# GpSimd computes the low halves of the down weights in the FFN stages and the experts, in place of VectorE

## The chip, the cores and the metric

The program runs on one NeuronCore of a Trainium2 chip. The metric is the device time of one execution in microseconds (us), taken as the median over several executions. TensorE is called PE here, VectorE DVE, ScalarE ACT, GpSimd POOL, and SP is the engine whose queue issues most of the loads.

## The reference

Two transformer-like blocks run one after the other over 256 tokens of width 1024. What matters here is their feed-forward part, which occurs four times as one dense FFN (twice in layer 0 of the first block, for the tokens and for the context; once in its layer 1; once in the second block) and once as a mixture of eight experts.

```python
def swiglu(h, wg, wu, wd):                      # FFN_DIM = 2816, in the second block 3584
    return (jax.nn.silu(h @ wg) * (h @ wu)) @ wd

def moe_swiglu(h, router_w, w_gate, w_up, w_down):
    ...
    top_v, top_i = lax.top_k(logits, TOP_K)
    top_p = jax.nn.softmax(top_v, axis=-1)
    gates = jnp.sum(jax.nn.one_hot(top_i, N_EXPERTS) * top_p[..., None], axis=1)
    for e in range(N_EXPERTS):                  # 8 experts, each 1024 -> 3584 -> 1024
        out = out + gates[:, e:e + 1] * swiglu_2(t, w_gate[e], w_up[e], w_down[e])
```

All inputs are fp32.

## The kernel before

**Chunks.** The hidden dimension of an FFN is cut into chunks of 128. One chunk needs 1.5 MB of fp32 weights: 128x1024 of the gate matrix, 128x1024 of the up matrix (together the "front" of a ring slot, 1 MB) and 128x1024 of the down matrix (the "back", 512 KB). The ring `RING` (in the trace: `weights`) has four slots. SP loads front and back in turn, and waits before each for the semaphore `front_used` or `back_used`, which says that the slot's old content has been read for the last time. The FFNs have 22, 22, 22 and 28 chunks, 94 together; the experts have 28 chunks each, 224 together.

**Splitting.** PE does not multiply the fp32 weights. Each is written as a sum of two bf16 numbers, high + low, and a product takes three bf16 passes (high x high, high x low, low x high). ACT makes the high half by a copy to bf16 (`cast_hi`; in the loops `cast_hi_loop`, lines 792 and 795), DVE the low half by subtracting the bf16 high half from the fp32 weights (`make_lo`): line 624 for gate and up together, 128x2048, and line 628 for down, 128x1024. The split weights have two buffers each, by the parity of the chunk. In the trace they are called `normed_or_mix` and `aux`.

**One step of the loop, chunk c.** PE does `up_products(c+1)` (lines 639 to 641, 48 matmuls), then `down_products(c)` (lines 654 to 656). In the experts the tokens of one expert are gathered to 128 columns, in the dense FFNs there are 256. ACT does the silu of chunk c (line 662), then the high half of gate and up of chunk c+2, then the high half of down of chunk c+1. DVE does `gate_of(c)`: the product of silu and up (line 669), its bf16 high half (line 677) and its low half (line 679); then `make_lo` of gate and up of chunk c+2, then `make_lo` of down of chunk c+1. `down_products(c)` waits for `back_used`, raised by the low half of down, and for `act_done`, raised by line 679. After 28 chunks of an expert DVE copies its output out of PSUM (`keep_output`, line 900) and PE adds it to the sum (line 852).

**Order.** Each engine's order is written out by hand, one instruction after another; there is no scheduler. The loop bodies hold four chunks, one for each ring slot. In the layout of the data line 624 and line 679 read two tensors from SBUF (weights and high half; hidden values and their high half), line 669 reads one from SBUF and one from PSUM, line 677 one from SBUF.

GpSimd has no instruction in these stages before the change. The experts are built twice, for up to 128 tokens in an expert (`moe_parts`) and for more (`ffn_parts` with gates), and a number counted on the chip chooses; in this case the first is run.

Of the kernel before, what the change touches and what calls it, by code (L numbers as in the profile page):

```python
# [21 lines left out]
ALU = mybir.AluOpType  # L22
# [3 lines left out]
D, T, PB = 1024, 256, 128  # L26
# [3 lines left out]
SLOT, SLOTS = KD * WC, 4  # L30
# [52 lines left out]
class Place:  # L83


    n = 0
# [57 lines left out]
def build(nc, ctx, d, out):  # L144
# [47 lines left out]
    S = Signals(sig)  # L192
# [426 lines left out]
    def make_lo(dve, which, j, n):  # L619

        s = (place.n + j) % SLOTS
        if which == 0:
            dve.wait_ge(S.hi_gu.sem, n + S.hi_gu.at(1))
            dve.tensor_tensor(gu[parity(j)][1], RING[:, s, 0:2 * D], gu[parity(j)][0],  # L624
                              ALU.subtract).then_inc(front_used.sem, 1)
        else:
            dve.wait_ge(S.hi_d.sem, n + S.hi_d.at(1))
            dve.tensor_tensor(split[parity(j)][2][1], RING[:, s, 2 * D:3 * D], split[parity(j)][2][0],  # L628
                              ALU.subtract).then_inc(back_used.sem, 1)

    def up_products(pe, j, n, hid, width, h_hi, h_lo):

# [49 lines left out]
    def ffn_done(n):  # L682
        place.n += n
        for s in (S.up_done, S.down_done, S.act_done, S.prod):
            s.done(n + 2)
        for s in (S.silu_done, S.act_hi, S.hi_gu, S.hi_d):
            s.done(n)

    def ffn_parts(x, f, o, gates=None):

        a, n = place.n, f // PB * (NE if gates is not None else 1)
        hid = [PS[:, 4 + p, :] for p in range(2)]
        h_hi, h_lo = (P[:, i * 1024:(i + 1) * 1024].bitcast(BF16).rearrange("p (k t) -> p k t", k=KD)
                      for i in range(2))
        h = HT[:, :, o:o + T]
        outs = ((0, (0, 1)), (1, (2, 3)))
        rounds = (n - 2) // SLOTS

        def products(pe):
            for bank in range(4):
                pe.matmul(PS[:, bank, :], Z16[:, 0:PB], Z16[:, :], start=True, stop=False)
            pe.sem_inc(S.up_done.sem, 2)
            pe.sem_inc(S.down_done.sem, 2)
            pe.wait_ge(S.hop_d.sem, S.hop_d.at(2))

            def up(j, n):
                up_products(pe, j, n, hid, T, lambda k: h_hi[:, k, :], lambda k: h_lo[:, k, :])
            up(0, 0)  # L710
            with pe.Fori(0, rounds) as g:
                for j in range(SLOTS):
                    up(j + 1, g * SLOTS + (j + 1))
                    down_products(pe, j, g * SLOTS + j, outs)
            for c in range(rounds * SLOTS, n):
                if c + 1 < n:
                    up(c + 1, c + 1)
                down_products(pe, c, c, outs, stop=(c == n - 1))

        def silus(act):  # L720
            act.activation(h_hi, h, ACT.Copy).then_inc(S.hop_d.sem, 1)
            cast_hi(act, 0, 0, 0)
            cast_hi(act, 0, 1, 1)
            cast_hi(act, 1, 0, 0)
            with act.Fori(0, rounds) as g:
                for j in range(SLOTS):
                    silu_of(act, j, g * SLOTS + j, hid, T)
                    cast_hi_loop(act, 0, j + 2, g, 0)
                    cast_hi_loop(act, 1, j + 1, g, 0)
            for c in range(rounds * SLOTS, n):  # L730
                silu_of(act, c, c, hid, T)
                if c + 2 < n:
                    cast_hi(act, 0, c + 2, c + 2)
                if c + 1 < n:
                    cast_hi(act, 1, c + 1, c + 1)

        def gating(dve):
            dve.sem_inc(S.act_done.sem, 2)
            dve.sem_inc(S.prod.sem, 2)
            dve.wait_ge(S.hop_d.sem, S.hop_d.at(1))  # L740
            dve.tensor_tensor(h_lo, h, h_hi, ALU.subtract).then_inc(S.hop_d.sem, 1)
            make_lo(dve, 0, 0, 0)
            make_lo(dve, 0, 1, 1)
            make_lo(dve, 1, 0, 0)
            if gates is None:
                with dve.Fori(0, rounds) as g:
                    for j in range(SLOTS):
                        gate_of(dve, j, g * SLOTS + j, hid, T)
                        make_lo(dve, 0, j + 2, g * SLOTS + (j + 2))
                        make_lo(dve, 1, j + 1, g * SLOTS + (j + 1))  # L750
                for c in range(rounds * SLOTS, n):
                    gate_of(dve, c, c, hid, T)
                    if c + 2 < n:
                        make_lo(dve, 0, c + 2, c + 2)
                    if c + 1 < n:
                        make_lo(dve, 1, c + 1, c + 1)
            else:
                fc = f // PB
                def steps(e, j, c, more=2):
                    gate_of(dve, j, c, hid, T, gates[:, bass.ds(e, 1), :].rearrange("p o t -> p (o t)"))  # L760
                    if more > 1:
                        make_lo(dve, 0, j + 2, c + 2)
                    if more > 0:
                        make_lo(dve, 1, j + 1, c + 1)
                with dve.Fori(0, NE - 1) as e:
                    with dve.Fori(0, fc // SLOTS) as g:
                        for j in range(SLOTS):
                            steps(e, j, e * fc + g * SLOTS + j)
                with dve.Fori(0, fc // SLOTS - 1) as g:
                    for j in range(SLOTS):  # L770
                        steps(NE - 1, j, g * SLOTS + ((NE - 1) * fc + j))
                for j in range(SLOTS):
                    steps(NE - 1, j, n - SLOTS + j, SLOTS - 1 - j)
            dve.wait_ge(S.down_done.sem, S.down_done.at(n + 2))
            for b in range(2):
                for h_ in range(2):
                    t = AUX[:, (2 * b + h_) * 512:(2 * b + h_ + 1) * 512]
                    dve_step(dve, dve.tensor_tensor(t, PS[:, 2 * b + h_, :], GB[:, h_ * 512:(h_ + 1) * 512], ALU.mult))
                    xo = x[:, b, h_ * 512:(h_ + 1) * 512]
                    dve.tensor_tensor(xo, xo, t, ALU.add)  # L780
        return products, silus, gating
# [15 lines left out]
    def ffn(x, f, o):  # L797

        a, n = place.n, f // PB
        products, silus, gating = ffn_parts(x, f, o)  # L800
        with nc.Block() as block:
            @block.sync
            def _(sp):
                feed(sp, a + SLOTS, a + n + SLOTS)

            @block.tensor
            def _(pe):
                products(pe)

            @block.scalar  # L810
            def _(act):
                silus(act)

            @block.vector
            def _(dve):
                gating(dve)
        ffn_done(n)
        S.hop_d.done(2)

    def moe_parts(he_hi, he_lo, put_t, fc):  # L820
# [69 lines left out]
        def gating(dve):  # L890
            def step(j, c, more=2):
                gate_of(dve, j, c, hid, PB)
                if more > 1:
                    make_lo(dve, 0, j + 2, c + 2)
                if more > 0:
                    make_lo(dve, 1, j + 1, c + 1)

            def keep_output(e):
                dve.wait_ge(S.down_done.sem, e * fc + S.down_done.at(fc + 2))
# [2 lines left out]
            dve.sem_inc(S.prod.sem, 2)  # L902
            make_lo(dve, 0, 0, 0)
            make_lo(dve, 0, 1, 1)
            make_lo(dve, 1, 0, 0)
            with dve.Fori(0, NE - 1) as e:
                with dve.Fori(0, fc // SLOTS) as g:
                    for j in range(SLOTS):
# [397 lines left out]
    for layer in range(2):  # L1306
# [476 lines left out]
        with nc.Block() as block:  # L1783
            @block.sync
            def _(sp):
                feed(sp, a + SLOTS, a + n + SLOTS)

            @block.tensor
            def _(pe):
                few = pe.value_load(COUNT[0:1, 0:1], min_val=0, max_val=T) <= PB  # L1790
                with pe.If(few):
                    gathered[0](pe)
                with pe.Else():
                    general[0](pe)

            @block.scalar
            def _(act):
                few = act.value_load(COUNT[0:1, 0:1], min_val=0, max_val=T) <= PB
                with act.If(few):
                    gathered[1](act)  # L1800
                with act.Else():
                    general[1](act)

            @block.vector
            def _(dve):
                few = dve.value_load(COUNT[0:1, 0:1], min_val=0, max_val=T) <= PB
                steps = dve_step.n
                with dve.If(few):
                    gathered[2](dve)
                dve_step.n = steps  # L1810
                with dve.Else():
                    general[2](dve)
        ffn_done(n)
        checkpoint(nc, "s1", X)

# [163 lines left out]
```

## Time and profile before

| | |
|---|---|
| median of 3 executions | 3390.8 us (3386.8 to 3391.04) |
| the profiled execution, its own time | 3383.39 us |
| its span, first to last instruction | 3381.6 us |
| mean granted TensorE clock | 0.893 |
| busy PE / DVE / ACT / POOL | 2904.6 / 1989.6 / 1411.8 / 0.2 us |
| experts, first to last line 624 | 2358.12 to 3344.36 us |
| HBM read | 674.71 MB |

The profile's rows give the start of an instruction, its duration, engine, line, operation, output<-inputs with their shapes, and in brackets how long the engine sat idle before it and what ended the idle time. Successive DVE instructions overlap by some 0.08 us in these rows, since one starts while the last results of the one before are written. So the distance from start to start says what an instruction costs its engine.

### The profile page before, as it was taken

How to read it: one execution, taken by the hardware profiler on the slowest of the kernel's cores; microseconds unless marked ns; L12 is line 12 of the kernel's file. 1: busy time of each engine (PE TensorE's matmuls, PEld its weight loads, DVE VectorE, ACT ScalarE, POOL GpSimd, SP SyncE). 2: the span in 40 equal slices, each digit the busy share in tenths (PEclk: the TensorE clock that was granted, in tenths of full speed). 3: DMA queues.
4: the chain of work that ended last, by engine and by line, in shares of the span. 5: the costliest groups of instructions: out<-in, count | busy, mean ns of one | idle time of the engine just before them, and what ended most of it. 6: DMA issues, size and time to landing. Idle time of an engine off the chain costs nothing. (4 is left out here: it accounts for less than half of the span.)

```text
span 3381.6 us, 59663 instructions
## 1 busy us (share of the span) xinstructions
PE 2904.6 (86%) x22985; PEld 2098.9 (62%) x23302; DVE 1989.6 (59%) x3126; ACT 1411.8 (42%) x1705; POOL 0.2 (0%) x4
## 2 busy tenths in 40 slices
PE   5879979999786777989668989767999999999997
PEld 3446657667453545766446766445777777777775
DVE  2234345555325553551446551445999999999997
ACT  1124124344123422430314430311777777777775
POOL 0000000000000000000000000000000000000000
PEclk8968789999887787999679999577999999999999
DMA  5440036455244204643424543320999999999995
GB/s 238 151 180 1 19 129 215 159 190 195 84 165 175 111 29 145 215 173 135 165 97 170 198 169 143 143 106 24 347 349 368 350 347 353 363 348 351 366 349 193
DMA packets 124090, 677.25 MB, mean 200 GB/s; under 512 B 13808, under 2 KB 14288, under 8 KB 69200
## 3 DMA queue, kind: packets, MB, share of 16 engines
q1 hardware_dynamic: 122256, 664.80, 53.0%
q10 hardware_dynamic: 1728, 11.01, 0.9%
q8 instruction: 70, 1.15, 0.1%
q14 instruction: 36, 0.29, 0.0%
HBM read 674.71 MB, written 1.05 MB: 200 GB/s over the span
## 5 line engine op out<-in xcount | busy, mean ns | idle before, releaser
L639 PE MATMUL ps<-projected,normed_or_mix 128*128 (+2 forms) x5088 | 1032.7, 236 | 46.8 <-DVE normed_or_mix L624 22.7
L640 PE MATMUL ps<-projected,normed_or_mix 128*128 (+2 forms) x5088 | 1030.5, 236 | 0.0
L639 PEld LDWEIGHTS ps<-projected,normed_or_mix 128*128 128x128 bf16 x5088 | 499.3, 98 | 173.5 <-DVE normed_or_mix L624 66.7
L792 ACT ACTIVATE normed_or_mix<-weights 128x2048 bf16<-128x2048 f32 x304 | 578.5, 1903 | 0.0
L640 PEld LDWEIGHTS ps<-projected,normed_or_mix 128*128 128x128 bf16 x5088 | 499.8, 98 | 33.0
L641 PE MATMUL ps<-projected,normed_or_mix 128*128 (+2 forms) x2544 | 519.0, 237 | 0.0
L641 PE MATMUL ps<-projected,aux 128*128 (+2 forms) x2544 | 510.9, 235 | 0.0
L551 PE MATMUL ps<-weights,turned 128*128 128x384 f32 (+3 forms) x1440 | 444.4, 472 | 17.7 <-PEq L420 7.2
L624 DVE TENSOR_TENSOR normed_or_mix<-weights,normed_or_mix 128x2048 bf16<-128x2048 f32 x159 | 364.0, 2289 | 48.9 <-ACT normed_or_mix L792 40.7
L551 PEld LDWEIGHTS ps<-weights,turned 128*128 128x128 f32 x1440 | 275.5, 194 | 185.9 <-issue 31.6
L624 DVE TENSOR_TENSOR aux<-weights,normed_or_mix 128x2048 bf16<-128x2048 f32 x159 | 363.7, 2287 | 28.2 <-ACT normed_or_mix L792 27.6
L662 ACT ACTIVATE probs<-ps 128x128 f32<-128x128 f32 (+1 forms) x318 | 97.8, 308 | 481.9 <-PE ps L641 481.1
L669 DVE TENSOR_TENSOR probs_turned<-probs,ps 128x128 f32<-128x128 f32 (+1 forms) x318 | 102.7, 323 | 269.1 <-ACT probs L662 269.1
L641 PEld LDWEIGHTS ps<-projected,normed_or_mix 128*128 128x128 bf16 x2544 | 251.1, 99 | 9.9
L641 PEld LDWEIGHTS ps<-projected,aux 128*128 128x128 bf16 x2544 | 248.9, 98 | 8.5
L628 DVE TENSOR_TENSOR aux<-weights,aux 128x1024 bf16<-128x1024 f32 x159 | 193.9, 1220 | 8.5 <-ACT aux L617 8.5
L628 DVE TENSOR_TENSOR normed_or_mix<-weights,normed_or_mix 128x1024 bf16<-128x1024 f32 x159 | 194.0, 1220 | 0.0
L335 PE MATMUL ps<-weights,silu_cond 128*32 128x384 f32 x1024 | 138.3, 684 | 43.6 <-DMA weights<-ada 14.5
L963 ACT ACT_TABLE_LOAD x30 | 38.5, 1283 | 322.7 <-PEq L537 203.5
L795 ACT ACTIVATE normed_or_mix<-weights 128x1024 bf16<-128x1024 f32 x152 | 159.9, 1052 | 19.6 <-PE ps L656 19.6
L795 ACT ACTIVATE aux<-weights 128x1024 bf16<-128x1024 f32 x152 | 159.4, 1049 | 11.1 <-PE ps L656 11.1
L655 PE MATMUL ps<-normed_or_mix,probs 128*128 128x512 bf16 x412 | 156.1, 379 | 8.6 <-DVE probs L679 0.3
(319 smaller groups left out, 3483.1 us busy)
## 6 DMA issues: line engine op xcount, KB each, us to landing
weights<-moe SPq DMA_DIRECT2D x224, 1024.0 KB, 7.1
weights<-moe SPq DMA_DIRECT2D x224, 512.0 KB, 7.2
weights<-l_ffn SPq DMA_DIRECT2D x66, 1024.0 KB, 5.1
weights<-ada SPq DMA_DIRECT2D x64, 1024.0 KB, 5.7
weights<-l_ffn SPq DMA_DIRECT2D x66, 512.0 KB, 5.5
weights<-ada SPq DMA_DIRECT2D x64, 512.0 KB, 6.5
weights<-ffn SPq DMA_DIRECT2D x28, 1024.0 KB, 4.9
weights<-w_in SPq DMA_DIRECT2D x16, 1024.0 KB, 5.8
```

Of the source, the lines that this page charges most:

```text
L335: mm = pe.matmul(PS[32 * j:32 * (j + 1), 5 + i % 2, 0:WC], CS[:, k, :], RING[:, (a + i) % SLOTS, k * WC:(k + 1) * WC], start=(turn_ == 0), ...
L551: mm = pe.matmul(PS[:, q % 8, 0:w], src(k)[:, b * PB:(b + 1) * PB], RING[:, slot, k * w:(k + 1) * w], start=(k == 0), stop=(k == kt - 1))
L624: dve.tensor_tensor(gu[parity(j)][1], RING[:, s, 0:2 * D], gu[parity(j)][0], ALU.subtract).then_inc(front_used.sem, 1)
L628: dve.tensor_tensor(split[parity(j)][2][1], RING[:, s, 2 * D:3 * D], split[parity(j)][2][0], ALU.subtract).then_inc(back_used.sem, 1)
L639: pe.matmul(o, hi, h_hi(k), start=(k == 0), stop=False)
L640: pe.matmul(o, hi, h_lo(k), start=False, stop=False)
L641: mm = pe.matmul(o, lo, h_hi(k), start=False, stop=(k == KD - 1))
L655: pe.matmul(PS[:, bank, :], hi[:, o], w_lo[:, c], start=False, stop=False)
L662: act.activation(silu[parity(j)][:, 0:width], hid[parity(j)][:, 0:width], ACT.Silu).then_inc(S.silu_done.sem, 1)
L669: dve.tensor_tensor(f, silu[p][:, 0:width], hid[p][:, T:T + width], ALU.mult).then_inc(S.prod.sem, 1)
L792: act.activation(gu[parity(j)][0], RING[:, s, 0:2 * D], ACT.Copy).then_inc(S.hi_gu.sem, 1)
L795: act.activation(split[parity(j)][2][0], RING[:, s, 2 * D:3 * D], ACT.Copy).then_inc(S.hi_d.sem, 1)
```

## The change

The low half of the down weights is made by GpSimd in a loop of its own (`down_lows`), with the same operands, buffers, semaphore waits and signals. DVE's `make_lo` keeps only gate and up. It applies to the four dense FFNs (`ffn`), and to the experts, in both their forms.

```diff
     def make_lo(dve, which, j, n):
 
         s = (place.n + j) % SLOTS
-        if which == 0:
-            dve.wait_ge(S.hi_gu.sem, n + S.hi_gu.at(1))
-            dve.tensor_tensor(gu[parity(j)][1], RING[:, s, 0:2 * D], gu[parity(j)][0],
-                              ALU.subtract).then_inc(front_used.sem, 1)
-        else:
-            dve.wait_ge(S.hi_d.sem, n + S.hi_d.at(1))
-            dve.tensor_tensor(split[parity(j)][2][1], RING[:, s, 2 * D:3 * D], split[parity(j)][2][0],
-                              ALU.subtract).then_inc(back_used.sem, 1)
+        dve.wait_ge(S.hi_gu.sem, n + S.hi_gu.at(1))
+        dve.tensor_tensor(gu[parity(j)][1], RING[:, s, 0:2 * D], gu[parity(j)][0],
+                          ALU.subtract).then_inc(front_used.sem, 1)
+
+    def down_lows(pool, n):
+        def low(j, c):
+            s = (place.n + j) % SLOTS
+            pool.wait_ge(S.hi_d.sem, c + S.hi_d.at(1))
+            pool.tensor_tensor(split[parity(j)][2][1], RING[:, s, 2 * D:3 * D], split[parity(j)][2][0],
+                               ALU.subtract).then_inc(back_used.sem, 1)
+
+        with pool.Fori(0, n // SLOTS) as g:
+            for j in range(SLOTS):
+                low(j, g * SLOTS + j)
+        for c in range(n // SLOTS * SLOTS, n):
+            low(c, c)
...
@@ -741,27 +749,21 @@
             make_lo(dve, 0, 0, 0)
             make_lo(dve, 0, 1, 1)
-            make_lo(dve, 1, 0, 0)
...
@@ -814,6 +816,10 @@
+
+            @block.gpsimd
+            def _(pool):
+                down_lows(pool, n)
...
@@ -892,8 +898,6 @@
                 gate_of(dve, j, c, hid, PB)
                 if more > 1:
                     make_lo(dve, 0, j + 2, c + 2)
-                if more > 0:
-                    make_lo(dve, 1, j + 1, c + 1)
```

In DVE's order at the experts before, the end of the prologue and the first step of the loop stand so (`probs` and `probs_turned` are the hidden values and their halves):

```order
L624 TENSOR_TENSOR normed_or_mix<-weights,normed_or_mix 128x2048
L624 TENSOR_TENSOR aux<-weights,normed_or_mix 128x2048
L628 TENSOR_TENSOR normed_or_mix<-weights,normed_or_mix 128x1024
L906 UNCONDITIONAL_BRANCH
L907 UNCONDITIONAL_BRANCH
L907 ISA
L669 TENSOR_TENSOR probs_turned<-probs,ps 128x128
L670 REGISTER_ALU
L676 REGISTER_ALU
L677 CAST probs<-probs_turned 128x128
L679 TENSOR_TENSOR probs<-probs_turned,probs 128x128
```

After the change the same place of DVE's order reads as follows; the new lines 623, 677, 685 and 687 are the old 624, 669, 677 and 679.

```order
L623 TENSOR_TENSOR normed_or_mix<-weights,normed_or_mix 128x2048
L623 TENSOR_TENSOR aux<-weights,normed_or_mix 128x2048
L909 UNCONDITIONAL_BRANCH
L910 UNCONDITIONAL_BRANCH
L910 ISA
L677 TENSOR_TENSOR probs_turned<-probs,ps 128x128
L678 REGISTER_ALU
L684 REGISTER_ALU
L685 CAST probs<-probs_turned 128x128
L687 TENSOR_TENSOR probs<-probs_turned,probs 128x128
L622 REGISTER_ALU
L623 TENSOR_TENSOR normed_or_mix<-weights,normed_or_mix 128x2048
```

The 128x1024 subtraction is gone from DVE, in the prologue and in each step, and nothing has taken its place. On POOL, which had no rows here, the loop of the experts is this:

```order
L633 ISA
L630 TENSOR_TENSOR normed_or_mix<-weights,normed_or_mix 128x1024
L629 REGISTER_ALU
L630 TENSOR_TENSOR aux<-weights,aux 128x1024
L629 REGISTER_ALU
L630 TENSOR_TENSOR normed_or_mix<-weights,normed_or_mix 128x1024
L629 REGISTER_ALU
L630 TENSOR_TENSOR aux<-weights,aux 128x1024
L633 REGISTER_ALU
L633 COMPARE_AND_BRANCH
```

So POOL holds all down subtractions of a stage, in the order of the chunks, and each waits only for ACT's high half of the same chunk.

## Rows read from the trace of the kernel before

**Rows 1.** The page's busy time, share of the span and instructions of each engine.

```profile
PE 2904.6 (86%) x22985; PEld 2098.9 (62%) x23302; DVE 1989.6 (59%) x3126; ACT 1411.8 (42%) x1705; POOL 0.2 (0%) x4
```

**Rows 2.** Busy time by window (dense FFN, experts), then clock, DMA share, GB/s.

```profile
500.00:560.00 60.00, 59.58 (x456) 45.17 (x462) 36.37 (x40) 28.22 (x27) 0.00 (x0) 1.00 0.58 203
...
2400.00:2480.00 80.00, 76.70 (x994) 59.58 (x1012) 76.40 (x96) 63.23 (x62) 0.00 (x0) 1.00 0.97 368
```

**Rows 3.** Timeline of DVE in the experts: one full step, and a later one.

```profile
2801.26 2.28 DVE L624 TENSOR_TENSOR normed_or_mix<-weights,normed_or_mix 128x2048 bf16<-128x2048 f32 x1
2803.46 1.22 DVE L628 TENSOR_TENSOR aux<-weights,aux 128x1024 bf16<-128x1024 f32 x1
2804.60 0.28 DVE L669 TENSOR_TENSOR probs_turned<-probs,ps 128x128 f32<-128x128 f32 x1
2804.91 0.23 DVE L677 CAST probs<-probs_turned 128x128 bf16<-128x128 f32 x1
2805.18 0.29 DVE L679 TENSOR_TENSOR probs<-probs_turned,probs 128x128 bf16<-128x128 f32 x1
2805.38 2.29 DVE L624 TENSOR_TENSOR aux<-weights,normed_or_mix 128x2048 bf16<-128x2048 f32 x1
...
2809.96 2.29 DVE L624 TENSOR_TENSOR normed_or_mix<-weights,normed_or_mix 128x2048 bf16<-128x2048 f32 x1 [0.28 <-ACT normed_or_mix L792]
```

**Rows 4.** Who waited for whom between 2400 and 3300 us: total, times, longest.

```profile
ACT probs L662 <- PE ps L641: 162.0, 109, 4.9
...
PEld ps L639 <- DVE normed_or_mix L624: 55.7, 80, 1.1
...
DVE normed_or_mix L624 <- ACT normed_or_mix L792: 15.6, 44, 0.7
```

**Rows 5.** Waits of SP's queue between 2400 and 3300 us.

```profile
SPq L226 <- DVE normed_or_mix L624: 274.9, 101, 3.8
```

**Rows 6.** Timeline of PE in the experts: two starts of up products, down products.

```profile
2799.48 0.23 PE L639 MATMUL ps<-projected,normed_or_mix 128*128 x1
...
2803.25 0.38 PE L656 MATMUL ps<-normed_or_mix,probs 128*128 128x512 bf16 x1
2803.60 0.23 PE L639 MATMUL ps<-projected,normed_or_mix 128*128 x1
...
2810.71 0.38 PE L655 MATMUL ps<-normed_or_mix,probs 128*128 128x512 bf16 x1
...
2812.31 0.23 PE L639 MATMUL ps<-projected,normed_or_mix 128*128 x1 [0.36 <-DVE normed_or_mix L624]
```

**Rows 7.** Timeline of DVE: the first and the last line 624 of the experts.

```profile
2358.12 2.29 DVE L624 TENSOR_TENSOR normed_or_mix<-weights,normed_or_mix 128x2048 bf16<-128x2048 f32 x1 [7.68 <-ACT normed_or_mix L614]
...
3344.36 2.28 DVE L624 TENSOR_TENSOR aux<-weights,normed_or_mix 128x2048 bf16<-128x2048 f32 x1
```

**Rows 8.** Timeline of DVE at the end of an expert.

```profile
2859.82 1.22 DVE L900 COPY aux<-ps 128x1024 f32<-128x1024 f32 x1
...
2867.94 0.29 DVE L669 TENSOR_TENSOR probs_turned<-probs,ps 128x128 f32<-128x128 f32 x1 [2.67 <-ACT probs L662]
...
2869.74 2.29 DVE L624 TENSOR_TENSOR aux<-weights,normed_or_mix 128x2048 bf16<-128x2048 f32 x1 [0.83 <-ACT normed_or_mix L792]
```

**Rows 9.** Timeline of ACT in the experts.

```profile
2804.35 1.05 ACT L795 ACTIVATE normed_or_mix<-weights 128x1024 bf16<-128x1024 f32 x1
2806.56 1.28 ACT L662 ACT_TABLE_LOAD   x1 [1.16 <-PE ps L641]
```

**Rows 10.** Timeline of DVE in a dense FFN: the halves of 256 columns.

```profile
512.72 0.29 DVE L677 CAST probs<-probs_turned 128x256 bf16<-128x256 f32 x1
513.05 0.43 DVE L679 TENSOR_TENSOR probs<-probs_turned,probs 128x256 bf16<-128x256 f32 x1
```

**Rows 11.** Window at the program's start: DMA share and GB/s last.

```profile
10.00:15.00 5.00, 2.56 (x16) 0.45 (x8) 0.00 (x0) 0.49 (x1) 0.00 (x0) 1.00 1.01 425
```

**Rows 12.** The page's DMA issues: KB each, median us to landing.

```profile
weights<-moe SPq DMA_DIRECT2D x224, 1024.0 KB, 7.1
```

More of the change, by code:

```diff
@@ L749, in gating @@
                         make_lo(dve, 0, j + 2, g * SLOTS + (j + 2))
-                        make_lo(dve, 1, j + 1, g * SLOTS + (j + 1))
                 for c in range(rounds * SLOTS, n):
@@ L754, in gating @@
                         make_lo(dve, 0, c + 2, c + 2)
-                    if c + 1 < n:
-                        make_lo(dve, 1, c + 1, c + 1)
             else:
@@ L894, in step @@
                     make_lo(dve, 0, j + 2, c + 2)
-                if more > 0:
-                    make_lo(dve, 1, j + 1, c + 1)
             def keep_output(e):
@@ L904, in gating @@
             make_lo(dve, 0, 1, 1)
-            make_lo(dve, 1, 0, 0)
             with dve.Fori(0, NE - 1) as e:
@@ L1812, in _ @@
                     general[2](dve)
+            @block.gpsimd
+            def _(pool):
+                down_lows(pool, n)
         ffn_done(n)
```

## The prediction

> **What bounds the kernel now.** I read the busy times by window first. In a dense FFN PE is busy 59.6 of 60 us and DVE 36.4; in the experts DVE is busy 76.4 of 80 us, PE 76.7, and the DMA share is 0.97 [rows 2]. So the two kinds of stage have different limits, and the reader should look at the experts, where three resources look full. The timeline of DVE settles which one it is: a step takes 4.12 us from line 624 to line 624, and DVE never stops in it: 2.20 us from line 624 to 628, 1.14 to 669, 0.31 to 677, 0.27 to 679, 0.20 to the next 624 [rows 3]. PE, in contrast, starts its up products at 2799.48 and again at 2803.60, and its last down matmul starts at 2803.25, some 0.22 us before PE could go on; its own work is 3.99 us of the 4.12 [rows 6]. The table of waits says the same: PE waits for DVE's line 624 80 times, ACT waits for PE, and nobody waits for a DMA [rows 4]. SP waits 274.9 us for line 624 [rows 5], so the ring is full of loads that arrive early and the high DMA share is a rate set by DVE. At the program's start the same queue moved 425 GB/s, at which 1.5 MB (1.57 million bytes) take 3.70 us [rows 11, 12].
>
> The mean distance of two lines 624 in the experts is more: 986.2 us over 223 steps, 4.42 us [rows 7]. Of the 0.30 us above 4.12, 0.14 come from ACT's table load: one step in four, the next line 624 comes 4.58 us after the one before, as 2805.38 + 4.58 = 2809.96, and the step in front of it takes 0.10 longer as well [rows 3, 9]. The remaining 0.16 us a step, 36 us in all, is what the ends of seven experts cost: the copy of 1.22 us and idle times of 2.67 and 0.83 us [rows 8].
>
> **What the change removes.** DVE loses 94 + 224 = 318 subtractions of 128x1024. In the dense FFNs PE has no gap to close, so their 94 are worth nothing. In the experts a step of DVE falls by 1.14 to 2.98 us.
>
> **What it adds.** The same subtraction on GpSimd, which computes nothing before (4 instructions, 0.2 us) [rows 1]. Its price is not in this trace. The lower bound is DVE's own 1.22 us [rows 3]. As upper bound I take twice that, 2.44 us, and as value 2.29 us, the time of the subtraction of twice the size on DVE [rows 3]; this is a choice, made near the upper end because nothing here shows GpSimd to be as fast as the engine made for such work.
>
> The Trainium skill, GPSIMD Engine Reference, section 3.1, gives 4497 ns for a 2048-column fp32 subtraction's sister, the add, on GpSimd, against 2293 ns on DVE; half of it is 2.25 us. DVE's 2.29 us for 2048 columns agrees; no run here shows GpSimd's. With 2.25 the sum below would be 9 us lower.
>
> **Where it lies.** If the two engines did not disturb each other, 2.29 us would be hidden. ACT finishes the down half at 2804.35 + 1.05 = 2805.40, and the down products that read it start at 2810.71 [rows 6, 9]: 5.31 us of room. The signal for the ring would come about a microsecond later than now, against loads that land 7.1 us after issue with four slots of over 4 us each [rows 12]; ACT has not waited for one.
>
> The open question is whether they disturb each other, and the trace has no place where both work. The bounds are 0 and the whole length of GpSimd's instruction in every step. Two things in the rows speak for the upper end. Lines 624 and 679, 2.49 of DVE's 2.98 us, read two tensors from SBUF. And line 677, which reads one, grows by only 0.06 us (0.23 to 0.29) for 128 more columns, where line 679 grows by 0.14 [rows 3, 10]: DVE has a second path into SBUF and uses it in both kinds. GpSimd must read two tensors too, from the same partitions. I take the upper end: while GpSimd's subtraction runs, lines 624, 677 and 679 wait, and the reverse.
>
> The Trainium skill, SBUF — State Buffer, section "Who interferes with whom", states just this: a DVE instruction with two SBUF inputs contends with a GpSimd instruction that reads SBUF, and the second to start blocks fully. No run here shows it yet. By it the change is slower; without it, faster (below).
>
> **The sum.** A step becomes 2.98 + 2.29 = 5.27 us. Line 669, which has one input in PSUM, could run beside GpSimd, which would give 4.96; but ACT issues the down half after gate and up (0.95 us later), so that GpSimd's turn comes late in line 624 or behind 669. I keep 5.27. The table load disappears: ACT already idles 1.16 us before it [rows 9], and with a step 1.15 us longer it fits. The ends of the experts keep their 36 us. So 223 x 5.27 + 36 = 1211 us in place of 986: +225 us. In a dense FFN DVE's step would be 2.98 + 0.35 (for 256 columns in place of 128, from line 679 and 677 and as much as line 679 again for line 669) + 2.29 = 5.6 us; PE needs 7.8 (60 us hold 7.7 such steps, with PE at 59.6 of 60), so the taking of turns is hidden under PE: 0. If that cover were gone, each 0.1 us a chunk would cost 9 us. Prologues: 0, since the first down subtraction has the first up products beside it.
>
> Against its own time of 3383.4 us this gives 3608; the median of the runs is 0.2% higher, which makes 3616. I say 3612 us, 6.5% slower.
>
> Bounds: with 2.44 us and 0.1 us for each of two hand-overs a step is 5.62 us and the sum +303, 3694 us. With 4.96 us a step it is +156, 3547. With GpSimd at 1.5 us it is 4.48 us a step and +49 to +80, depending on whether the table load is hidden, so about 3450.
>
> **The rivals.**
> *No disturbance, PE next.* DVE's 2.98 us fit easily, and PE sets 3.99 us a step. Once in four steps the table load shows: from its start at 2806.56, when PE had just finished its up products, to the start of the up products two chunks on, 2812.31, are 5.75 us [rows 6, 9], against 3.99 + 1.3 us of PE's own work between (down, up, down): 0.46 us, 0.12 a step. 223 x 4.11 + 36 = 953 us, -33: 3358 us, 1.0% faster. The load rate is no obstacle (3.70 us). For it: the 5.31 us of room. Against it: the second input of line 624.
> *GpSimd is the bound by itself,* undisturbed but slow. It decides from 4.26 us on (the mean step inside an expert now), and at 4.6 us costs 223 x 0.34, some +75 us: 3466. Against it: it is nearly four times DVE's time.
> *Partial disturbance, or a short GpSimd instruction.* At 1.22 us and taking turns a step is 4.20 us: +18 us, 3409. If GpSimd slipped into DVE's gaps and only stretched its instructions, the 1.14 us come back as about 1.14 us: no change.
>
> **How the numbers follow.** Taking turns at about 2.3 us: 0.72, with a range of its own from 3540 to 3700. Partial, or short: 0.08, of which 0.05 no change, the rest slower. GpSimd the bound: 0.04. PE next: 0.16. A measurement of this kernel can tell some 0.2% from no change. That makes faster 0.16, same 0.05, slower 0.79. The range goes from 3450 to 3710: it leaves out the faster case and most of the near-neutral ones.
>
> **What would show it.** Line 623 (now 624) starting every 5.0 to 5.6 us in the experts, with idle time or a longer duration on lines 623, 685 and 687 next to a GpSimd instruction; no start of one inside the other's run. PE's busy share there falls to about 3.99 of 5.3, and the DMA rate to near 300 GB/s. The dense FFNs keep 7.8 us a chunk. I am wrong if line 623 starts every 4.0 us with GpSimd running beneath it; or if GpSimd's instructions come back to back.

## The result, and the profile after

The changed kernel takes 3501.4 us (median of 4 runs, 3500.1 to 3508.0) against 3390.9 us before: a ratio of 1.0331, 95% interval 1.0305 to 1.0357, 110 us slower. The forecast was slower, 3612 us in a range of 3450 to 3710. The direction and the mechanism held; the size was twice what was measured.

First the page after, busy time by engine and the lines that answer to the ones shown of before (line 623 is the old 624, 677 the old 669, 685 the old 677, 687 the old 679).

```profile
PE 2909.9 (83%) x22985; PEld 2119.8 (61%) x23302; DVE 1977.1 (56%) x2808; ACT 1416.6 (40%) x1705; POOL 1016.2 (29%) x322
...
L630 POOL TENSOR_TENSOR normed_or_mix<-weights,normed_or_mix 128x1024 bf16<-128x1024 f32 x159 | 455.4, 2864 | 1962.7 <-ACT normed_or_mix L617 1661.4
L630 POOL TENSOR_TENSOR aux<-weights,aux 128x1024 bf16<-128x1024 f32 x159 | 562.5, 3537 | 487.6 <-ACT aux L797 458.6
```

The same trace's groups, with the shapes kept apart, give the cast of the experts alone:

```profile
L685 DVE CAST probs<-probs_turned 128x128 bf16<-128x128 f32 x224 | 266.9, 1191 | 17.3
```

DVE has 318 instructions fewer, and yet it is busy for 1977.1 us, 12.5 us less than before, where 318 x 1.14 = 363 us were taken away. Its cast of 128 columns, which took 0.23 us [rows 3], has a mean of 1191 ns. Its work did not grow; the cast waits inside its own span.

The windows of the same stretches as in [rows 2] show where the loss is.

```profile
500.00:560.00 60.00, 59.58 (x452) 44.69 (x458) 28.74 (x32) 28.22 (x27) 23.73 (x8) 1.00 0.59 209
2400.00:2480.00 80.00, 64.61 (x849) 51.31 (x864) 68.33 (x65) 53.24 (x53) 45.58 (x17) 1.00 0.84 314
```

In the dense FFN PE is as busy as before, 59.58 of 60 us. In the experts PE falls from 76.70 to 64.61 of 80 us and the loads from 368 to 314 GB/s. From its first to its last line 623 the experts' stage takes 3459.89 - 2367.27 = 1092.6 us, where it took 986.2 [rows 7]: +106.4 us, nearly the whole difference.

The timeline of DVE and of POOL in the experts, one round of four steps, shows the mechanism instruction by instruction.

```profile
2800.14 2.29 DVE L623 TENSOR_TENSOR aux<-weights,normed_or_mix 128x2048 bf16<-128x2048 f32 x1 [0.84 <-ACT normed_or_mix L794]
2802.35 0.28 DVE L677 TENSOR_TENSOR probs_turned<-probs,ps 128x128 f32<-128x128 f32 x1
2802.66 1.85 DVE L685 CAST probs<-probs_turned 128x128 bf16<-128x128 f32 x1
2804.54 0.29 DVE L687 TENSOR_TENSOR probs<-probs_turned,probs 128x128 bf16<-128x128 f32 x1
2804.75 2.28 DVE L623 TENSOR_TENSOR normed_or_mix<-weights,normed_or_mix 128x2048 bf16<-128x2048 f32 x1
2806.95 0.28 DVE L677 TENSOR_TENSOR probs_turned<-probs,ps 128x128 f32<-128x128 f32 x1
2807.27 1.85 DVE L685 CAST probs<-probs_turned 128x128 bf16<-128x128 f32 x1
2809.15 2.20 DVE L687 TENSOR_TENSOR probs<-probs_turned,probs 128x128 bf16<-128x128 f32 x1
2811.27 2.28 DVE L623 TENSOR_TENSOR aux<-weights,normed_or_mix 128x2048 bf16<-128x2048 f32 x1
...
2814.34 2.28 DVE L623 TENSOR_TENSOR normed_or_mix<-weights,normed_or_mix 128x2048 bf16<-128x2048 f32 x1
```

```profile
2801.13 3.29 POOL L630 TENSOR_TENSOR normed_or_mix<-weights,normed_or_mix 128x1024 bf16<-128x1024 f32 x1 [6.83 <-ACT normed_or_mix L797]
2805.11 3.93 POOL L630 TENSOR_TENSOR aux<-weights,aux 128x1024 bf16<-128x1024 f32 x1 [0.68 <-ACT aux L797]
2809.08 2.12 POOL L630 TENSOR_TENSOR normed_or_mix<-weights,normed_or_mix 128x1024 bf16<-128x1024 f32 x1
2814.44 4.18 POOL L630 TENSOR_TENSOR aux<-weights,aux 128x1024 bf16<-128x1024 f32 x1 [3.24 <-ACT aux L797]
```

Read the ends, not the starts. GpSimd's second instruction is issued at 2805.11, inside line 623, which ends at 2807.03; it ends at 2809.04, 2.01 us after line 623. Beside it line 677 runs in its usual 0.28 us. The cast, issued at 2807.27, ends at 2809.12, right behind GpSimd. GpSimd's third subtraction was ready by then (ACT's high half of it ended at 2809.01) and is issued at 2809.08, ahead of DVE's line 687, which ends at 2811.35, behind GpSimd's 2811.20. This third one, which had nothing to wait for, gives GpSimd's own time: 2.12 us. The two engines take turns by whole instructions, and line 677, with one input in PSUM, is exempt. The Trainium skill, SBUF — State Buffer, section "Who interferes with whom", states that rule for two-input instructions and for casts at double rate; the trace agrees on both.

The steps from line 623 to line 623 in this round are 4.61, 6.52, 3.07 and 4.60 us. The second holds two of GpSimd's turns, the third none. This pattern repeats in the experts 2 to 8, with 18.72 us for most rounds; the first expert has another, shown further down. PE waits for DVE in all this and not for GpSimd itself: between 2400 and 3300 us its down products wait 70.2 us for line 687, and GpSimd's line 630 released PE's weight load once in the whole trace, after 1.7 us. No engine waits for a load there.

### The profile page after: what moved, and what is told of

Same layout as the page of the kernel before. It is cut to its first block and busy times, and to the rows that moved or that the text cites. A ratio compares the mean times of both kernels' runs of the same rounds, so it can differ in the third digit from the quotient of the medians.

```text
span 3499.7 us, 60146 instructions
## 1 busy us (share of the span) xinstructions
PE 2909.9 (83%) x22985; PEld 2119.8 (61%) x23302; DVE 1977.1 (56%) x2808; ACT 1416.6 (40%) x1705; POOL 1016.2 (29%) x322
## 5 line engine op out<-in xcount | busy, mean ns | idle before, releaser
L630 POOL TENSOR_TENSOR normed_or_mix<-weights,normed_or_mix 128x1024 bf16<-128x1024 f32 x159 | 455.4, 2864 | 1962.7 <-ACT normed_or_mix L617 1661.4
L630 POOL TENSOR_TENSOR aux<-weights,aux 128x1024 bf16<-128x1024 f32 x159 | 562.5, 3537 | 487.6 <-ACT aux L797 458.6
L623 DVE TENSOR_TENSOR normed_or_mix<-weights,normed_or_mix 128x2048 bf16<-128x2048 f32 x159 | 390.7, 2457 | 37.6 <-ACT normed_or_mix L794 29.2
L685 DVE CAST probs<-probs_turned 128x128 bf16<-128x128 f32 (+1 forms) x318 | 299.0, 940 | 23.4
L663 PE MATMUL ps<-aux,probs 128*128 128x512 bf16 x412 | 156.2, 379 | 89.2 <-DVE probs L687 84.0
L687 DVE TENSOR_TENSOR probs<-probs_turned,probs 128x128 bf16<-128x128 f32 (+1 forms) x318 | 206.2, 648 | 10.9
```

What stands on the lines that cost most here:

```text
L630: pool.tensor_tensor(split[parity(j)][2][1], RING[:, s, 2 * D:3 * D], split[parity(j)][2][0], ALU.subtract).then_inc(back_used.sem, 1)
L663: pe.matmul(PS[:, bank, :], hi[:, o], w_lo[:, c], start=False, stop=False)
L685: dve.tensor_copy(hid_hl[p][0][:, 0:width], f).then_inc(S.act_hi.sem, 1)
L687: dve.tensor_tensor(hid_hl[p][1][:, 0:width], f, hid_hl[p][0][:, 0:width], ALU.subtract).then_inc(S.act_done.sem, 1)
```

## The experiments

Twelve kernels were run, each beside runs of the kernel before on the same chip; the ratio is taken against those. "Step" is the distance of two of DVE's 128x2048 subtractions in the experts, "stage" the stretch from the first to the last of them, before 986.2 us. The stage is the sharper measure, since the program ahead of it varies: the experts begin anywhere between 2357 and 2391 us in the profiles, with no order by kernel.

**One column.** GpSimd keeps its place and its signals, but subtracts only one column; the low half of the other 1023 is set to zero once ahead of each stage's loop.

```diff
-            pool.tensor_tensor(split[parity(j)][2][1], RING[:, s, 2 * D:3 * D], split[parity(j)][2][0],
-                               ALU.subtract).then_inc(back_used.sem, 1)
...
+            w_hi, w_lo = split[parity(j)][2]
+            pool.tensor_tensor(w_lo[:, 0:1], RING[:, s, 2 * D:2 * D + 1], w_hi[:, 0:1], ALU.subtract).then_inc(back_used.sem, 1)
...
+        for p in range(2):
+            pool.memset(split[p][2][1][:, 1:D], 0.0)
```

> The kernel after the change, but GpSimd subtracts only column 0 of the down weights; the other 1023 columns of the low half stay zero, so that part of the product is left out. All waits and signals between the engines stay. Theory (the two engines take turns, GpSimd's work of 2.0 us is the price): with nothing to take turns over, PE is next, 4.0 to 4.1 us a step in the experts, 3350 to 3370 us. Rival (the way over GpSimd, its waits and signals, costs the time): still 3450 to 3500 us.

Measured: 3366.4 us, ratio 0.9926 (0.9900 to 0.9952), stage 961.6 us. The loss is gone with GpSimd's columns, so it is not the way over GpSimd. This is also the nearest measurement of the forecast's rival in which PE is next: it gave -33 us, the run shows -24.6 us in the stage. Even an instruction of one column takes its turn, as two rows of this run's timeline show:

```profile
2799.35 2.29 DVE L623 TENSOR_TENSOR aux<-weights,normed_or_mix 128x2048 bf16<-128x2048 f32 x1 [0.90 <-ACT normed_or_mix L796]
```

```profile
2800.34 1.35 POOL L631 TENSOR_TENSOR normed_or_mix<-weights,normed_or_mix 128x1 bf16<-128x1 f32 x1 [2.62 <-ACT normed_or_mix L799]
```

It is issued at 2800.34 and ends at 2801.69, just behind line 623, which ends at 2801.64.

**A write, a cast.** Behind the one column GpSimd fills the other 1023 with zeros, or casts the fp32 weights into them.

```diff
+            pool.memset(w_lo[:, 1:D], 0.0).then_inc(back_used.sem, 1)
```

> As the one-column kernel, but GpSimd then writes zeros to the other 1023 columns: a long GpSimd instruction that writes SBUF and reads none; the low half is left out of the product. Theory in its form that only reads collide with two-input instructions: lines of DVE's 128x2048 subtraction and of the hidden low half are not lengthened; DVE's cast, which runs at twice the rate, may be, by up to the length of the write (1 us or so). 3350 to 3400 us. Rival (any GpSimd work holds DVE): DVE's 128x2048 subtraction starts late too, 3420 us or more.

```diff
+            pool.tensor_copy(w_lo[:, 1:D], RING[:, s, 2 * D + 1:3 * D]).then_inc(back_used.sem, 1)
```

> As the one-column kernel, but GpSimd then casts the other 1023 columns of the fp32 weights to bf16 into the low half, one input in place of two; the low half of the product is wrong by that. Theory: it reads SBUF, so it and DVE take turns as in the changed kernel, for as long as it runs; a one-input instruction should be shorter, 1.0 to 1.3 us, so a step of 3.0 - 0.3 + 1.2 = 3.9 us is under PE's 4.0: 3355 to 3410 us, with the cast and the low half of DVE lengthened. Rival (two GpSimd inputs are what collides): no DVE instruction is lengthened.

Measured: 3368.8 us (0.9925, 0.9900 to 0.9951) and 3365.3 us (0.9918, 0.9886 to 0.9950). The write takes 0.94 us and the cast 1.03 us, and both fit under PE (stages of 961.8 and 961.7 us). DVE's cast waits for either, in 161 of the 224 steps of the experts. In the run with the write:

```profile
2803.90 0.78 DVE L686 CAST probs<-probs_turned 128x128 bf16<-128x128 f32 x1
```

```profile
2803.65 0.94 POOL L632 MEMSET aux<- 128x1023 bf16 x1
```

The cast ends at 2804.68, GpSimd's write at 2804.59. So against DVE's cast at double rate GpSimd need not read anything. Whether DVE's two-input subtraction would have let the write or the one-input cast pass was not seen: both always began when it had ended, since the one column in front of them had waited for it. That part of the two expectations stays untested.

**The high half from PSUM.** The changed kernel, with DVE's cast replaced by a product that reads PSUM; and as a control the kernel before with the same edit.

```diff
+        if gate is None:
+            dve.wait_ge(S.down_done.sem, n + S.down_done.at(1))
+            dve.tensor_tensor(hid_hl[p][0][:, 0:width], silu[p][:, 0:width], hid[p][:, T:T + width],
+                              ALU.mult).then_inc(S.act_hi.sem, 1)
...
-        dve.wait_ge(S.down_done.sem, n + S.down_done.at(1))
-        dve.tensor_copy(hid_hl[p][0][:, 0:width], f).then_inc(S.act_hi.sem, 1)
```

> The kernel after the change, but in the dense FFNs and the experts DVE makes the bf16 high half of the hidden values by a second product of silu (SBUF) and up (PSUM) in place of the cast from SBUF; same values. Theory: an instruction with one SBUF input that is not at double rate passes beside GpSimd, so only line 687's 0.2 us and the 128x2048 subtraction's 2.2 us take turns with GpSimd's 2.0: steps of 4.4 us in place of 4.6, 3440 to 3475 us, although DVE has 0.05 us more work a step. Rival (GpSimd holds every DVE instruction, or slows all by bandwidth): 3500 to 3515 us.

> The kernel before with the bf16 high half of the hidden values made from silu and PSUM in place of the cast, as in the run before that did so with GpSimd. Theory: DVE's step grows by 0.05 us or less, 3390 to 3405 us, so that the 3547 us of that run are due to how DVE and GpSimd meet, not to the other instruction by itself. Rival (the second product is costly by itself): 3430 us or more.

Measured: 3546.6 us (1.0464, 1.0413 to 1.0514), a clear miss, and for the control 3381.0 us (0.9960, 0.9926 to 0.9994). The rows of the run with GpSimd tell what was right and what was not:

```profile
2872.86 0.28 DVE L679 TENSOR_TENSOR probs<-probs,ps 128x128 bf16<-128x128 f32 x1
2873.05 0.28 DVE L681 TENSOR_TENSOR probs_turned<-probs,ps 128x128 f32<-128x128 f32 x1
2873.37 1.71 DVE L692 TENSOR_TENSOR probs<-probs_turned,probs 128x128 bf16<-128x128 f32 x1
2875.01 4.21 DVE L623 TENSOR_TENSOR aux<-weights,normed_or_mix 128x2048 bf16<-128x2048 f32 x1
```

```profile
2871.64 3.30 POOL L630 TENSOR_TENSOR aux<-weights,aux 128x1024 bf16<-128x1024 f32 x1 [2.04 <-ACT aux L802]
2874.89 2.18 POOL L630 TENSOR_TENSOR normed_or_mix<-weights,normed_or_mix 128x1024 bf16<-128x1024 f32 x1
```

Both products with PSUM pass beside GpSimd unhindered, and the step that meets one turn of GpSimd is 4.36 us, as expected (4.4). But most rounds are 4.36 + 6.27 + 4.62 + 5.33 = 20.6 us. The 6.27 us are a matter of order: GpSimd's next subtraction was ready before its last one had ended, was issued at 2874.89 and went ahead of line 623, which took 4.21 us, and line 623 is what PE waits for. In the step of 5.33 us the table load is exposed: DVE idles 1.33 us ahead of its first product.

The step of 4.62 us has another cause, TensorE's clock. PE idled 2.13 us, until line 623 ended, and started its up products at 2879.28. Half a microsecond later the granted clock in PE's rows is 0.50, the level of 1.2 GHz, and a matmul takes 0.31 us in place of 0.22; by 2884.80 it is back at 1.00, 2.4 GHz. The windows show it (PEclk is the number behind the brackets of POOL):

```profile
2879.80:2883.00 3.20, 3.20 (x33) 3.20 (x31) 3.20 (x2) 0.00 (x0) 1.41 (x1) 0.50 0.81 266
2884.80:2887.50 2.70, 2.70 (x49) 2.61 (x47) 1.72 (x2) 2.02 (x2) 0.60 (x1) 1.00 0.90 291
```

In the experts of this run 1272 up matmuls took more than 0.28 us; in every other run 26 to 56 did, all in the first expert. In each expert at least one round with the same order of turns but no slow matmul in its first step takes 19.33 us; those with them take 20.58. So the clock costs 1.25 us a round, in 31 of the 55 rounds: an estimate of 39 us, the ends of the experts left aside. That leaves some 3508 us for the order of the turns, still above the expected 3475. The expectation had neither: the sum of a step alone does not give the time.

The order is not a matter of this edit alone. The first expert of the changed kernel has it too: GpSimd goes ahead of line 623, and a step later DVE idles for the table load.

```profile
2427.97 4.22 DVE L623 TENSOR_TENSOR normed_or_mix<-weights,normed_or_mix 128x2048 bf16<-128x2048 f32 x1
2436.81 0.29 DVE L677 TENSOR_TENSOR probs_turned<-probs,ps 128x128 f32<-128x128 f32 x1 [1.63 <-ACT probs L670]
```

```profile
2427.83 2.22 POOL L630 TENSOR_TENSOR aux<-weights,aux 128x1024 bf16<-128x1024 f32 x1 [2.90 <-ACT aux L797]
```

There a round is 20.05 us in place of 18.72, with PE at full clock. What puts one expert in one pattern and the next in the other is not shown. The control shows that the edit itself is a gain: DVE's steps are 4.06 us, where 4.12 to 4.17 were expected, as the second product starts 0.20 us after the first where the cast started 0.31 us after it.

**Each stage alone.** The change in the experts only, and in the dense FFNs only (`down_lows` in one kind of stage, `make_lo` for both halves in the other).

> The change in the experts alone; the dense FFNs keep the down subtraction on DVE. Theory (the loss is in the experts, where DVE has no room): as the changed kernel, 3490 to 3510 us. Rival (part of the loss is in the dense FFNs or in loading GpSimd's code there): some 10 us or more below it.

> The change in the four dense FFNs alone. Theory: GpSimd takes turns with DVE there as well, but under PE's 7.8 us a chunk: as before within 0.2%, 3384 to 3398 us, with the cast lengthened all the same. Rival: the difference of 9 us ahead of the experts between the two profiles is real and belongs to the FFNs, 3400 us or more.

Measured: 3499.9 us (1.0269, 1.0209 to 1.0329), and 3391.9 us (0.9979, 0.9946 to 1.0013). The stages are 1092.4 and 986.4 us, so all of the loss belongs to the experts. The expectation and the prediction had DVE held in the dense FFNs as well, with PE's longer work covering it. It is hardly held at all: in the changed kernel one cast of 94 takes 1.77 us (at 504.01) and three more are longer than 0.30, and no other line of DVE's loop is lengthened; it is GpSimd that waits, 2.7 us being its usual duration in place of 2.12. DVE is idle 24 of 60 us there even before [rows 2], and GpSimd's turns fall into that time. The stretches from the first to the last 128x2048 subtraction are 351.7, 157.9 and 205.6 us against 351.7, 158.2 and 204.5 before (the first holds two FFNs).

**Two halves.** Each of GpSimd's subtractions is cut into two of 128x512.

```diff
...
+            pool.tensor_tensor(w_lo[:, 0:512], RING[:, s, 2 * D:2 * D + 512], w_hi[:, 0:512], ALU.subtract)
+            pool.tensor_tensor(w_lo[:, 512:D], RING[:, s, 2 * D + 512:3 * D], w_hi[:, 512:D],
                                ALU.subtract).then_inc(back_used.sem, 1)
```

> The changed kernel with each of GpSimd's subtractions cut into two of 128x512. Theory: the turn is per instruction, so DVE never waits longer than about 1.05 us for one GpSimd instruction where it now waits up to 1.9; the sum of GpSimd's time stays, 2.0 to 2.2 us a step, so the total stays within 3470 to 3530 us. Rival (bandwidth shared, no turns): no change in how DVE's instructions are lengthened.

Measured: 3467.7 us (1.0178, 1.0119 to 1.0237), just under the expected interval, stage 1058.9 us. DVE's waits have the new length:

```profile
2802.46 0.87 DVE L687 CAST probs<-probs_turned 128x128 bf16<-128x128 f32 x1
2803.36 1.15 DVE L689 TENSOR_TENSOR probs<-probs_turned,probs 128x128 bf16<-128x128 f32 x1
2804.44 3.25 DVE L623 TENSOR_TENSOR aux<-weights,normed_or_mix 128x2048 bf16<-128x2048 f32 x1
```

The cast waits 0.64 us, the low half 0.86, line 623 0.97. A turn is an instruction, and cutting it gives DVE places to get in.

**A share for GpSimd.** DVE subtracts the first 896, or 512, of the 1024 columns and its signal starts GpSimd on the rest, so that GpSimd's turn falls on the product from PSUM.

```diff
+            dve.tensor_tensor(w_lo[:, 0:896], RING[:, s, 2 * D:3 * D - 128], w_hi[:, 0:896],
+                              ALU.subtract).then_inc(S.lo_d.sem, 1)
...
+            pool.wait_ge(S.lo_d.sem, c + S.lo_d.at(1))
+            pool.tensor_tensor(w_lo[:, 896:D], RING[:, s, 3 * D - 128:3 * D], w_hi[:, 896:D],
+                               ALU.subtract).then_inc(back_used.sem, 1)
```

> GpSimd subtracts only the last 128 of the 1024 columns of the down weights, in all stages, and starts when DVE has done the first 896, so that its turn falls on line 669's product, which reads one input from PSUM and passes beside it. Theory: GpSimd's instruction takes 0.3 to 0.35 us, DVE's step falls from 4.12 to between 3.98 and 4.1 us, where PE's 3.99 takes over: 3366 to 3392 us. Rival (any use of GpSimd here costs more than it gives): 3395 us or more.

> As the run with 128 columns, with 512 of the 1024 on GpSimd. Theory: GpSimd's instruction takes 1.0 to 1.1 us, of which 0.3 lie beside the product from PSUM; DVE's step is 2.98 + 0.6 + 0.8 = 4.4 us, some 60 us more than before in the experts less up to 31 us of table loads that become hidden: 3415 to 3460 us. Rival (no turns, GpSimd hidden): below 3375 us.

Measured: 3387.6 us (0.9986, 0.9974 to 0.9998), steps of 4.12 us, stage 980.9 us, and 3432.0 us (1.0121, 1.0100 to 1.0143), steps of 4.45 us with no table load to be seen, stage 1022.1 us. With 512 columns GpSimd's 1.16 us lengthen most casts from 0.23 to 1.00 us or more; what DVE saves by the columns, 0.54 us, is less. With 128 nearly all of the 0.14 us saved is used up: GpSimd's 0.43 us reach past the product, and nine casts in ten have 0.27 to 0.36 us. A round is 16.95 us where it was 17.04, the 5 us of the stage.

**Both.** The share and the product from PSUM together, with 128 and with 256 columns on GpSimd.

> GpSimd subtracts the last 128 columns of the down weights, started by DVE's first 896, and DVE makes the bf16 high half of the hidden values from silu and PSUM in place of the cast. Theory: GpSimd's instruction of 0.43 us now lies beside two products that read PSUM, 0.5 us together, and costs DVE at most 0.1 us; DVE's step is 4.06 - 0.14 + 0.08 = 4.0 us, at PE's 3.99. With the table loads as in the one-column kernel: 3362 to 3376 us, faster than the kernel before and than the control without GpSimd (3381 us). Rival (a share for GpSimd gives nothing even so, as with 128 columns and the cast): 3378 to 3395 us.

> As the run with 128 columns and the product from PSUM, with 256 columns on GpSimd. Theory: GpSimd takes 0.65 us and begins 0.15 us after the first product, so that 0.3 us stick out and hold the low half; DVE's step is 4.06 - 0.28 + 0.3 = 4.08 us, no better than the control without GpSimd: 3372 to 3390 us, slower than 128 columns. Rival (turns cost little for short instructions): as fast as 128 columns or faster.

Measured: 3368.5 us (0.9951, 0.9929 to 0.9972) and 3368.8 us (0.9930, 0.9910 to 0.9950). Both beat the kernel before; the two cannot be told apart, and 256 columns did better than expected. With 128:

```profile
2805.15 0.28 DVE L687 TENSOR_TENSOR probs<-probs,ps 128x128 bf16<-128x128 f32 x1
2805.35 0.28 DVE L689 TENSOR_TENSOR probs_turned<-probs,ps 128x128 f32<-128x128 f32 x1
2805.66 0.29 DVE L700 TENSOR_TENSOR probs<-probs_turned,probs 128x128 bf16<-128x128 f32 x1
```

```profile
2805.31 0.43 POOL L638 TENSOR_TENSOR aux<-weights,aux 128x128 bf16<-128x128 f32 x1 [4.44 <-DVE aux L630]
```

GpSimd's subtraction lies from 2805.31 to 2805.74 under the two products, and line 700 still has its usual 0.29 us. The steps are 3.93 us three times in four, with 4.87 for the one with the table load; with 256 columns line 700 has 0.47 us and the steps are 3.97 us, with 4.73. A round is 16.66 us in both, and the same with one column: DVE's turns with GpSimd no longer set it, and that is why 256 columns are no worse. The stages are 965.6 and 966.5 us, against 975.5 in the control and 961.6 with one column. So GpSimd's share is worth some 10 us of stage beyond the product from PSUM; in the whole time, measured on different chips, the intervals of the two kernels and of the control overlap, and that part is shown only by the profiles.

## Why the prediction was right, and its size was not

**What bounds the experts** was right: DVE. Taking 1.14 us a step from it without putting anything in its way gained 24.6 us (one column), and PE then set the pace. (Lines 624 and 679 are 2.40 of the 2.98 us from start to start, not 2.49; nothing hangs on it.)

**The dense FFNs at nothing** was right, by the run with them alone, but not by the route of the prediction: DVE's step does not grow by GpSimd's 2.29 us there, since the turns fall into DVE's idle time (4 of 94 casts are lengthened).

**The range** held 3501.4 us, but not for the reason it was drawn for. Turns at about 2.3 us had a range of their own, 3540 to 3700, and the measured time lies below it. What caught it is the lower end of 3450, put there for a GpSimd that takes 1.5 us; it takes 2.12.

**The turns** were right: lines 685, 687 and 623 wait for GpSimd's whole instruction, and GpSimd for theirs. From the cast's small growth with its columns the prediction inferred a second path into SBUF. The runs show what was concluded from it, that the cast waits, even against a write, while the product with an input in PSUM does not; the path itself they do not show. Two signs were wrong. "No start of one inside the other's run" fails in the rows above, since the record of an instruction begins when it is issued and contains its wait. And GpSimd's instructions coming back to back was given as evidence against the forecast. They do come so once in a round, and it is the costliest step, 6.4 us.

**The failed size is the step of 5.27 us**, as "2.98 + 2.29"; the mean in most of the experts is 18.72 / 4 = 4.68 us. The mis-sized term is the turn, 2.29 us. In the rows above a step with one turn is 4.61 us, so the turn costs 1.63. It ends 2.01 us after line 623, not 2.29 (GpSimd takes 2.12 by itself). And 0.38 of the 2.01 us lie beside DVE's work: line 669, now 677, and the beginning of the cast. The prediction had said that line 669 does not lie beside GpSimd ("I keep 5.27"), on the ground that ACT delivers the down half late. It is late, inside line 623, and for that very reason GpSimd starts when line 623 ends, with line 677 beside it. The second turn of a pair has no such cover: from line 687 to the next line 623 are 2.12 us in place of 0.20, a cost of 1.92. Three turns at 1.63 and one at 1.92 are 1.70 in the mean, and 2.98 + 1.70 = 4.68 us. Over 223 steps the 0.59 us make 132 us less.

**The ends of the experts** were kept at 36 us; what is left of the stage beside 223 x 4.68 us is 49 us, 13 more. 225 - 132 + 13 = 106 us, the stage's measured loss. But 8 of the 13 us are not ends: they are six rounds of the first expert, each 1.33 us longer. The table load was rightly taken as hidden in the experts 2 to 8, and is exposed in the first.

**The rival of no disturbance** was priced at -33 us and the run nearest to it gives -24.6. What the table load costs is more than was worked out: with one column the round is 3.08 + 4.27 + 3.98 + 5.33 = 16.66 us, where 4 x 4.11 = 16.44 were assumed.

## What to carry to other kernels

In these runs work given from DVE to GpSimd was parallel where DVE was idle or its instructions at that time had an operand in PSUM; beside two-input subtractions from SBUF or the cast at double rate it was serial, at 2.12 us where DVE takes 1.22. Before such a move, add GpSimd's instruction to DVE's step, take off only what reads PSUM, and look which DVE instruction it will go ahead of, since a turn in front of the one that PE waits for costs more than the sum says. Look at PE's clock as well where its waits grow. A small share, started by DVE's own signal just in front of its PSUM instructions, was the form that gained, once two such instructions stood there; beside one it gave 5 us of the stage.

## What the runs showed of the hardware

GpSimd's subtraction (fp32 minus bf16 to bf16, 128 partitions) took 0.43, 0.67, 1.16 and 2.12 us for 128, 256, 512 and 1024 columns when its turn was free: some 1.9 ns a column and 0.19 us fixed, by the first and the last. A write of 1023 bf16 columns took 0.94 us, a cast from fp32 1.03 us.

After a wait of 2.13 us TensorE began at its full clock and fell to the level of 1.2 GHz 0.5 us later, for some 3 us, in the run with the high half from PSUM. In the same run a wait as long near the start of each expert is followed by the full clock, and in the changed kernel PE idled at most 2.0 us between 2400 and 3300 us and kept it. What decides between the two is not shown.

The record of an instruction that waits for its turn contains the wait: GpSimd's busy time of 1016.2 us on the page is more than 318 x 2.12 = 674 us of work, and DVE's busy time hid the loss in the same way. Nothing in the table of waits names it either. It is seen only where one form's durations spread (the cast: 0.23 to 1.86 us) and its ends fall on the other engine's ends.
